# Transformer block pair on one core: norms rescaled by other engines, weight loads moved up in their queue, TensorE groups reordered

## The reference

```python
# first block
h = rms_norm(x, mix_norm_g) @ w_in              # q, k, v, 8 gates, z
attn = forgetting_attention(q, k, v, log_sigmoid(f + b_f))
sgu = spatial_gating(gelu(z), ...)              # gated unit over 128 positions
x = x + concat(rms_norm(attn), rms_norm(sgu)) @ w_out
gate, up = split(rms_norm(x, ffn_norm_g) @ w_gate_up)
x = x + (silu(gate) * up) @ w_down
x = rms_norm(x, final_norm_g)
# second block, with 256 context tokens
k_c, v_c = split(modulate(rmsnorm(ctx)) @ w_in_2[kv])
q, k, v, u, b, c, ga, gc = split(modulate(rmsnorm(x)) @ w_in_2)
o = latent_window_attention(rope(q), rope(k), v, k_c, v_c, sink)
y = b * conv3(c * u)
x = x + g1 * (sigmoid(ga) * (o @ w_proj_attn) + sigmoid(gc) * (y @ w_proj_conv)) @ w_out_2
h2 = modulate(rmsnorm(x))                       # router: 16 experts, 128 tokens each
x = x + g2 * expert_choice_moe(h2, ...)
out = rmsnorm(x, final_norm_g_2)
```

## Time and profile before

| | |
|---|---|
| median of 3 runs | 3060.75 us (3056.59 to 3062.23) |
| the profiled execution's own time | 3061.53 us |
| its span in the trace | 3059.5 us |
| mean granted TensorE clock | 0.969 |
| busy: TensorE, weight load, DVE, ACT, POOL | 93%, 74%, 58%, 43%, 17% |
| HBM traffic over the span | 437 MB, 143 GB/s |

### The profile page before, as it was taken

How to read it: one execution, slowest core, us unless ns; L and a number is a source line. 1 busy time by engine, 2 the same in 40 slices (tenths; PEclk the granted TensorE clock), 3 DMA queues, 4 the chain that set the end, 5 groups by cost and what they waited for, 6 DMA issues and landing times.

```text
span 3059.5 us, 34754 instructions
## 1 busy us (share of the span) xinstructions
PE 2856.7 (93%) x14050; PEld 2273.1 (74%) x14050; DVE 1759.6 (58%) x2356; ACT 1303.1 (43%) x1814; POOL 532.9 (17%) x432
## 2 busy tenths in 40 slices
PE   5999988999999899899999999999999489999994
PEld 4777767788778788788887666766778368888883
DVE  3344534788775233843323455554445669999995
ACT  5344433333333223311111666664223257777773
POOL 1011112555554000321000111111000200000001
PEclk8999989999999999999999999999999789999997
DMA  3210122245654421221211111114334569999994
GB/s 124 63 42 28 42 83 89 90 138 152 186 151 171 171 94 51 78 72 42 76 55 49 42 40 37 39 42 145 96 108 160 219 253 390 392 398 397 398 386 153
DMA packets 239476, 439.27 MB, mean 144 GB/s; under 512 B 27421, under 2 KB 134053, under 8 KB 238805
## 3 DMA queue, kind: packets, MB, share of 16 engines
q1 hardware_dynamic: 217184, 359.69, 33.5%
q0 software_dynamic: 21984, 77.33, 7.4%
q10 hardware_dynamic: 148, 0.04, 0.0%
HBM read 383.43 MB, written 53.58 MB: 143 GB/s over the span
## 4 chain that ended last, share of the span: by engine, by line
PE 85%; DVE 7%; ACT 3%; DMA 2%; issue 2%; POOL 1%; SPq 0%; ACTq 0%; DVEq 0%; POOLq 0%
PE PS L125 80%; PE PS L128 5%; DVE m L134 3%; ACT m L131 2%; DVE m L140 1%; DMA m<-in_w_down_dram 1%; POOL m L134 1%; DVE m L143 1%; ACT L131 0%; DVE m L176 0%; DVE m L179 0%; DVE m L173 0%; DMA m<-in_w_proj_attn_dram 0%; DMA m<-xa_scratch 0%; DMA m<-in_w_proj_conv_dram 0%
## 5 line engine op out<-in xcount | busy, mean ns | idle before, releaser
L125 PE MATMUL PS<-m,m 128*128 128x512 f32 (+4 forms) x12234 | 2665.8, 391 | 56.2 <-DVE m L134 38.3
L125 PEld LDWEIGHTS PS<-m,m 128*128 128x128 f32 (+2 forms) x12234 | 2065.5, 184 | 581.6 <-issue 117.6
L134 DVE TENSOR_TENSOR m<-m,m 128x2048 fp32r<-128x2048 f32 (+5 forms) x574 | 851.1, 1503 | 445.7 <-ACT m L131 417.2
L131 ACT ACTIVATE m<-m 128x2048 fp32r<-128x2048 f32 (+5 forms) x602 | 701.3, 1180 | 929.6 <-PE PS L125 437.9
L131 ACT ACTIVATE m<-PS 128x512 f32<-128x512 f32 (+4 forms) x503 | 280.4, 578 | 526.9 <-PE PS L125 342.0
L134 DVE TENSOR_TENSOR m<-PS,m 128x512 fp32r<-128x512 f32 (+1 forms) x360 | 236.6, 684 | 300.1 <-PE PS L125 249.6
L134 POOL TENSOR_TENSOR m<-m,m 128x512 f32<-128x512 f32 (+3 forms) x169 | 273.0, 1618 | 674.6 <-DVE small L143 219.3
L128 PE MATMUL PS<-ident,m 128*128 128x128 f32 (+1 forms) x1592 | 229.7, 284 | 107.2 <-DVE m L149 36.0
L128 PEld LDWEIGHTS PS<-ident,m 128*128 128x128 f32 (+1 forms) x1592 | 197.3, 147 | 146.5 <-DVE m L149 36.2
L131 ACT ACTIVATE m<-m,small 128x640 f32<-128x640 f32 (+5 forms) x203 | 161.6, 797 | 221.1 <-DVE small L137 154.9
L143 DVE CUSTOM_DVE_ANT_0 m<-PS,m 128x640 f32<-128x640 f32 (+4 forms) x192 | 146.4, 775 | 120.1 <-PE PS L125 120.1
(11 more groups left out here) (79 smaller groups left out, 468.2 us busy)
## 6 DMA issues: line engine op xcount, KB each, us to landing
m<-in_w_exp_gate_dram SPq DMA_DIRECT2D x64, 1024.0 KB, 8.7
m<-in_w_exp_up_dram SPq DMA_DIRECT2D x64, 1024.0 KB, 8.9
m<-in_w_exp_down_dram SPq DMA_DIRECT2D x64, 1024.0 KB, 8.2
m<-in_w_mod_dram SPq DMA_DIRECT2D x48, 512.0 KB, 3.7
m<-in_w_gate_up_dram SPq DMA_DIRECT2D x44, 512.0 KB, 6.4
m<-in_w_in_dram SPq DMA_DIRECT2D x41, 512.0 KB, 4.1
m<-in_w_in_dram SPq DMA_DIRECT2D x12, 1024.0 KB, 5.1
h_scratch<-m POOLq DMA_DIRECT2D x22, 512.0 KB, 3.6
```

The lines of the kernel that those rows point to most:

```text
L125: return Unsent() if self.e is None else self.e.matmul(o, l, r, start=first, stop=last, **k)
L131: return Unsent() if self.e is None else self.e.activation(o, i, fn, **k)
L134: return Unsent() if self.e is None else self.e.tensor_tensor(o, a, b, op)
```

## The change

The first norm goes by pairs of tiles: ACT squares whole tiles, DVE alone scales, and the splits of a pair follow those of the next pair's squares. Piece 0 is split before the last pair's parts, piece 1 after them. TensorE begins `W_QK[0]` with the two groups that need only tokens 0 to 511. The sqrt table is loaded first.

```diff
-            for h0 in (0, 4):
-                for i in range(h0, h0 + 4):
+            act.wait_ge("masks", "one")
+            act.activation(tab, one, ACT.Sqrt).then_inc(*act.did("act_table"))
+            for j in range(4):
+                for i in (2 * j, 2 * j + 1):
                     act.wait_ge(f"x_in{i}", "x")
-                    for j in range(2):
-                        square(act, X[:, i, half512(j)], ssq[:, i, j:j + 1], "x", i, j)
-                root_of(act, ssum[:, h0:h0 + 4], "x", h0 // 4)
...
+                    square(act, X[:, i, :], ssum[:, i:i + 1], "x", i, junk=x_junk)
+                root_of(act, ssum[:, 2 * j:2 * j + 2], "x", j)
+                if j:
+                    x_highs(act, j - 1)
+            w_high(act, 0)
+            x_highs(act, 3)
+            w_high(act, 1)
...
+            for j in range(4):
+                dve.wait_ge("act_junk~", "x", 2 * j + 1)
+                mean_of(dve, ssum[:, 2 * j:2 * j + 2], 1024, "x", j)
+                inverse_of(dve, ssum[:, 2 * j:2 * j + 2], rs8[:, 2 * j:2 * j + 2], "x", j)
+                dve.wait_ge("rstd", "x", j)
+                for i in (2 * j, 2 * j + 1):
+                    dve.tensor_scalar(X[:, i, :], X[:, i, :], rs8[:, i:i + 1], None, ALU.mult).then_inc(*dve.did("x_scaled", i))
+                if j:
+                    x_lows(dve, j - 1)
...
+            w_low(dve, 0)
+            x_lows(dve, 3)
+            w_low(dve, 1)
...
         def in_pe(pe):
+            for g in (0, 3):
+                feat_group(pe, W_QK[0], Q1_ORDER[g][0], 0, xrhs, "q1_acc", (g,), q1_out(g))
             pe.wait_ge("x_low", 7, 4)
             feat_group(pe, W_F, 0, 1, xrhs, "f_acc", (1,), ("f_out", 1))
-            for g, (what, h) in enumerate(Q1_ORDER):
-                feat_group(pe, W_QK[0], what, h, xrhs, "q1_acc", (g,), q1_out(g))
+            for g in (1, 2):
+                feat_group(pe, W_QK[0], Q1_ORDER[g][0], 1, xrhs, "q1_acc", (g,), q1_out(g))
```

```diff
+            for i in range(0, NT, 2):
+                act.wait_ge("rstd", "zu", i // 4)
+                act.activation(zu[:, i, :], zu[:, i, :], ACT.Copy, scale=rs8[:, i:i + 1]).then_inc(*act.did("zu_scaled_a", i))
             w_high(act, W_O + 1)
             for i in range(NT):
-                if zu_scaler(i) == "ACT":
...
                 act.wait_ge("zu_turned", i)
```

Loads before and in the down projection; `x1` comes back later:

```diff
             for m in range(2, 6):
                 h_load(sp, m)
+            w_load(sp, W_DN + 2)
             sp.wait_ge("gu_acc", 21, "P4")
             sp.wait_ge("h_st0", 20)
             sp.wait_ge("h_st1", 21)
-            for m in range(6, 11):
+            h_load(sp, 6)
+            h_load(sp, 7)
+            w_load(sp, W_DN + 3)
+            for m in range(8, 11):
                 h_load(sp, m)
...
             pool.wait_ge("gu_acc", 21, "P3")
+            pool.wait_ge("h_low", 5)
```

```diff
+                        if i >= 4:
+                            md_high(act, *md_parts[i - 4], hch)
                         act.wait_ge("x2_half", 1, i)
...
-                        if i == 5:
+                        if i == 7:
                             h2_root(act, 0)
-                        if i >= 4:
-                            md_high(act, *md_parts[i - 4], hch)
...
+                        if c and i >= 4:
+                            md_low(dve, *md_parts[i - 4], hch, hcl)
                         if c and i:
                             h2_sum(dve, 1, i - 1)
-                        if (c, i) == (1, 4):
+                        if (c, i) == (1, 6):
                             h2_mean(dve, 0)
-                        if c and i >= 4:
-                            md_low(dve, *md_parts[i - 4], hch, hcl)
-                        if (c, i) == (1, 6):
-                            h2_inverse(dve, 0)
-                            modulate_dve(dve, 0)
+            h2_inverse(dve, 0)
+            modulate_dve(dve, 0)
```

```diff
-                if s:
+                if s > 1:
                     gate_part(pe, s, 0, 2)
...
+                if s == 0:
+                    gate_part(pe, 1, 0, 4)
...
             w_load(sp, W_PA + 1)
+            w_load(sp, W_PA + 2)
             for n in range(4):
                 gate_load(sp, n)
             for n in range(32):
-                if n and n < 16 and n % 2 == 0:
-                    w_load(sp, W_PA + n // 2 + 1)
-                if n >= 16 and n % 4 == 0:
-                    w_load(sp, W_PC + (n - 16) // 4 + 1)
+                if n < 16 and n % 2 == 0:
+                    w_load(sp, W_PA + n // 2 + 3)
+                if n in (16, 20):
+                    w_load(sp, W_PC + n // 4 - 1)
                 gate_load(sp, n + 4)
...
             for h in range(2):
+                if h:
+                    w_low(dve, W_PA + 1)
                 for k in range(8):
                     dve.wait_ge("o2_high", h, k)
...
-        ROUTE = [("out", 0, 0, 0, 8), ("out", 1, 0, 0, 8), ("out", 2, 0, 0, 8), ("out", 0, 1, 0, 8), ("norm", 0),
+        ROUTE = [("out", 0, 0, 0, 4), ("out", 1, 0, 0, 4), ("out", 2, 0, 0, 4), ("out", 0, 0, 4, 8), ("out", 1, 0, 4, 8),
+                 ("out", 2, 0, 4, 8), ("out", 0, 1, 0, 8), ("norm", 0),
```

```diff
             for j in range(4):
-                i = 2 * j
-                act.wait_ge(f"x_in{i}", "f")
-                act.wait_ge("act_junk~")
-                act.activation(xf_junk[0], XF[:, i, :], ACT.Square, accum_out=ssum[:, i:i + 1]).then_inc(*act.did("act_junk~", "f", i))
-                root_of(act, ssum[:, i:i + 2], "f", j)
-                if j < 3:
-                    act.wait_ge("rstd", "f", j)
-                    act.activation(XF[:, i, :], XF[:, i, :], ACT.Copy, scale=rs8[:, i:i + 1]).then_inc(*act.did("xf_scaled", i))
+                for i in (2 * j, 2 * j + 1):
+                    act.wait_ge(f"x_in{i}", "f")
+                    square(act, XF[:, i, :], ssum[:, i:i + 1], "f", i, junk=xf_junk)
+                root_of(act, ssum[:, 2 * j:2 * j + 2], "f", j)
...
-                for t in range(i + (j < 3), i + 2):
+                for t in (i, i + 1):
                     dve.scalar_tensor_tensor(XF[:, t, :], XF[:, t, :], rs8[:, t:t + 1], fg, ALU.mult, ALU.mult).then_inc(
                         *dve.did("y_out_f", t))
```

More of the change, by code:

```diff
@@ L492, in xlhs @@
             return xh[:, k, tile128(i)], xl[:, k, tile128(i)]
-        def scaler(i):
-            return "DVE POOL ACT".split()[i % 3]
+        x_junk = ar(64, 1024)
         def setup_sp(sp):
@@ L513, in setup_pool @@
             pool.memset(one, 1.0).then_inc(*pool.did("masks", "one"))
-            for i in range(NT):
-                if scaler(i) == "POOL":
-                    pool.wait_ge("rstd", "x", i // 4)
-                    pool.tensor_scalar(X[:, i, :], X[:, i, :], rs8[:, i:i + 1], None, ALU.mult).then_inc(*pool.did("x_scaled_p", i))
-        def x_scaled(i):
-            return {"DVE": "x_scaled_v", "POOL": "x_scaled_p", "ACT": "x_scaled_a"}[scaler(i)], i
         def setup_act(act):
@@ L950, in zu_scaler @@
         def zu_scaler(i):
-            return "POOL ACT DVE".split()[i % 3]
+            return "ACT DVE".split()[i % 2]
         def zu_scaled(i):
-            return {"ACT": "zu_scaled_a", "DVE": "zu_scaled_v", "POOL": "zu_scaled_p"}[zu_scaler(i)], i
+            return {"ACT": "zu_scaled_a", "DVE": "zu_scaled_v"}[zu_scaler(i)], i
         def mlhs(k, i):
@@ L1178, in merge_pool @@
         def merge_pool(pool):
-            for i in range(NT):
-                if zu_scaler(i) == "POOL":
-                    pool.wait_ge("rstd", "zu", i // 4)
-                    pool.tensor_scalar(zu[:, i, :], zu[:, i, :], rs8[:, i:i + 1], None, ALU.mult).then_inc(*pool.did("zu_scaled_p", i))
             pool.wait_ge("zu_low", 7)
@@ L1544, in ffn_sp @@
             sp.wait_ge("h_st1", 21)
-            for m in range(6, 11):
+            h_load(sp, 6)
+            h_load(sp, 7)
+            w_load(sp, W_DN + 3)
+            for m in range(8, 11):
                 h_load(sp, m)
         def down_sp(sp):
-            for n in range(W_DN + 2, W_K2 + 1):
+            for n in range(W_DN + 4, W_K2 + 1):
                 w_load(sp, n)
@@ L2470, in proj_act @@
             for h in range(2):
+                if h:
+                    w_high(act, W_PA + 1)
                 for k in range(8):
@@ L2473, in proj_act @@
                     act.activation(oh[:, k, half512(h)], q2[:, k, half512(h)], ACT.Copy).then_inc(*act.did("o2_high", h, k))
-            for n in range(8):
+            for n in range(1, 8):
                 w_high(act, W_PA + n + 1)
@@ L2495, in proj_dve @@
             for n in range(16):
-                if n % 2 == 0:
+                if n and n % 2 == 0:
                     w_low(dve, W_PA + n // 2 + 1)
@@ L2995, in final_sp @@
             for i in range(NT):
-                sp.wait_ge(*last_out(i))
+                sp.wait_ge("y_out_f", i)
                 sp.dma_start(out[0, tile128(i), :], XF[:, i, :]).then_inc(*sp.landed("out_st"))
             sp.wait_ge("out_st")
```

(4 more changed lines are left out.)

79 lines of the change are left out of this document (27 added, 52 removed).

## The result

| | before | changed |
|---|---|---|
| median (runs of one comparison) | 3061.49 us (3056.59 to 3063.21) | 3015.47 us (3014.61 to 3016.39) |
| span of the profiled execution | 3059.5 us | 3012.7 us |
| mean granted TensorE clock | 0.969 | 0.975 |

The changed kernel takes 0.9852 of the time of the one before (95% interval 0.9835 to 0.9869), 46 us less. The forecast was 3014.

What follows compares the result with a forecast made beforehand. TensorE, busy 2856.7 of 3059.5 us, was taken as the bound, with idle and half-clock time to win. Eight added terms gave 47.2 us, taking 3061.53 to 3014.3, adjusted and rounded to 3014; range 3003 to 3030.

Steps and rivals of the forecast that it cites:

- its rivals: Whole kernel: small inputs don't come, 3032 us (0.14); down projection fails, 3024 (0.05); clock takes it back, 3077 (0.03).
- its small input: Rival, each stage: a late input hides another a few us earlier; 29 us gained in all, 3032 us; chance 0.14.
- First norm: Start of the kernel: `W_QK[0]` starts at 42.2 instead of 51.68; 9.5 less 2.0 for half clock, 7.5 us gained.
- 7.19 as before since the clock is at half there too: First norm: the 24 matmuls of `W_F` keep their 7.19 us, taken to be at half clock already.
- Gated unit: Eight transpose groups from 429.42: scalings done beforehand, four cycles end at 438.3 instead of 445.76; 7.5 us gained.
- I leave that loss in: Gated unit: the 54 matmuls behind the transposes still lose 2.2 us to half clock; without it the term is 9.7.
- Down projection: Third piece of `w_down` lands near 990, so TensorE's 8.08 us halt and 2.3 of slow clock go; 10.4 us.
- Context: Keys start at 1240.7 instead of 1245.73, but DVE bounds the stage from there; 2.0 us, bounds 0 and 5.
- second attention: Step 1's 12 gate matmuls fill 4.11 idle us; the next halt ends about 1.3 earlier; 1.3 us, bounds 0 and 3.
- Projections and output projection: Earlier weight loads and splits remove halts and slow clock, 9.1 us; 36 matmuls cover the split of `W_O2 + 1`, 3.6.
- End: Final norm: DVE's last scaling at 3048.4 instead of 3054.75, less 0.5 for the queue; 5.8 us, bounds 3.5 and 7.5.
- Share the queue and take back 0.5: End: 8 MB of loads and stores on one queue cost 0.5 us of the gain.

Runs made afterwards that it cites:

- the kernel with this part alone: The kernel before with only the changed kernel's first norm: 3052.42 us, 7.4 less.
- either of its two parts: The kernel before with only SP's load order ahead of the down projection changed: 3048.96 us; with only the return of x1 delayed: 3051.11 us.
- The part alone: The kernel before with only the gated unit's scalings moved ahead of the split of `W_O + 1`: 3051.89 us, 7.9 less.
- the two executions of the changed kernel: The changed kernel as first measured, 3015.47 us, and run once more unchanged, 3013.81 us; one profiled execution of each.
- the undone part: The changed kernel with the end of the kernel before (DVE squares odd tiles, ACT and POOL finish even ones): 3019.91 us.
- one line: The changed kernel with the first half of `W_F`'s product behind the transposes of tiles 6 and 7: 3005.07 us.
- four others: The changed kernel with second-norm sums ahead of the modulation (3012.3 us), the end ahead of the last expert in two forms (3012.96, 3011.58), or the earlier end (3019.91).
- seven traces: The kernel before, the changed kernel twice, its earlier end, two forms of an end ahead of the last expert, and three edits together (3005.49 us).

## Why the prediction was right

- **The method held**: the sum was 47.2, the trace has 46.8. None of its rivals came: every place brought more than its small input, the down projection lost its halt, and the mean clock went up (0.969 to 0.975). That the total came so near is luck in part: the terms brought 4.1 us more than forecast in three places (2.05 behind the gated unit, 1.9 in the projections, 0.2 in the down projection) and 4.5 less in seven others, losses of clock that the forecast didn't have among them.
- **First norm**, 7.5: 7.0. The start of `W_F` was forecast 1.6 too late and its length 1.4 too short, which cancelled. "7.19 as before since the clock is at half there too" was the wrong step: 24 matmuls in 7.19 us are not at half clock, and they took 8.63 here and 7.54 in the kernel with this part alone. `W_QK[0]` began 9.0 us sooner, and 2.0 went back as forecast, in 312 matmuls that took 73.01 us instead of 71.02.
- **Gated unit**, 7.5: 7.4 to the resumption, and 2.05 more since the clock stayed up. The term took the loss over from the kernel before. The step that failed is "I leave that loss in". The Trainium skill (TensorE: Matmul & The Clock Gate, on transposes) says that transposes don't count as busy; by it the loss was to stay. The part alone agrees, where the clock fell to 0.50 among the transposes; the two executions of the changed kernel don't, where it stayed at 1.00 through 9 us of them and behind.
- **Down projection**, 10.4: 10.6. Right in size; the runs showed that either of its two parts would have brought it.
- **Context**, 2.0: 1.5; **second attention**, 1.3: 0.8. Both were named as limited by what comes next, and that came: DVE beside POOL in one, waits of 1.35 and 2.11 us in the other. In the context the values came 1.2 us sooner, where the keys came 5.4 sooner. In the second attention the halts gave 2.3 us, and the clock took 1.6 back behind the last of them: six matmuls took 2.83 us instead of 1.66 and eight transposes 1.49 instead of 1.03.
- **Projections and output projection**, 12.7: 14.6. The halts went as said. The 1.9 us more are 0.6 of idle time (a wait of 0.17 us was left where 0.8 was reckoned) and 1.4 of matmuls: the 912 took 5.65 us less where 4.2 was reckoned, since they ran at 0.227 us and not 0.229.
- **End**, 5.8: 4.7, by the undone part 4.4 to 6.1. The last scaling ends at 3006.6, 6.1 us before the span does, where it was 4.8 before. "Share the queue and take back 0.5" was the step that was mis-sized: with DVE faster the DMA engines are full (1.02) and SP had its last store 5.9 us behind the last scaling, where it was 3.7. That is 2.2 us more, less the 1.0 us for which the kernel before had waited for POOL's queue to close, a wait that the forecast didn't have and that went with POOL's additions.
- **Not foreseen**: 1.25 us lost on the way to the down projection and 0.6 in the first experts, both in stretches that start with TensorE at the other clock level (264 matmuls in 61.90 us instead of 60.30 at the feed-forward's start). The second profiled execution of the changed kernel lost the first again and somewhat more, and not the second. A fall of the clock in a dense stretch had been named as a sign of being wrong; it showed in small (0.94 for 555 to 560 us, 0.85 for 1660 to 1665). These losses cancel with the gated unit's 2 us, so the total looks better than its terms.

## What to carry to other kernels

Follow one piece of work through both traces and book the lead stage by stage: here every place came out within 2.1 us of its forecast, and errors that cancel become visible. When a wait has two causes that come together, remove them one at a time: the cheaper may be enough. After a reorder, look at once for the engine that now stands longest; the 11 us of ACT in the changed kernel's first norm were worth 9 us for one line. And look at who holds the end: POOL's queue took 7.5 us and more to close, so an instruction of POOL at the very end of a kernel costs what the last transfer doesn't cover (another engine's queue in its place was not tried).

## What the runs showed of the hardware

- The granted clock behind a break can come out either way with the same instructions: the eight groups of transposes took 9.0 us in both executions of the changed kernel and 9.46 to 10.18 in four others with the same instructions up to there, and the matmuls behind them started at a granted clock of 1.00 or of 0.50 (2.4 or 1.2 GHz).
- DVE beside POOL: a 128x2048 subtraction took 4.50 us instead of 2.29, two additions of 128x4 2.29 instead of 0.23, and POOL's own pair of additions 7.78 instead of 6.16. Moving one instruction out of POOL's way puts the next one into it.
- POOL's queue closed 7.5 to 8.3 us after the end of POOL's last instruction (DRAINs of 8.75 to 10.95 us in seven traces), and no kernel's span ended before that. A write by index of 128 rows to the output, 0.5 MB, had landed 3.3 us after the start of its issue.
- With loads and stores mixed the DMA engines moved 416 to 421 GB/s when their busy share was 1.02 to 1.03, and 201 GB/s at 0.50 in the old end.
